# RWKV scan: the triangular inverse computed in 32x32 blocks instead of 64x64

## The reference, cut to what matters

```python
def rwkv7_scan(r, decay, k, v, kk, b, reverse):
    def step(S, inp):
        r_t, w_t, k_t, v_t, kk_t, b_t = inp
        sa = jnp.einsum('bhij,bhj->bhi', S, -kk_t)
        S = (S * w_t[:, :, None, :] + sa[..., None] * b_t[:, :, None, :]
             + v_t[..., None] * k_t[:, :, None, :])
        return S, jnp.einsum('bhij,bhj->bhi', S, r_t)
    S0 = jnp.zeros((B, H, N, N), r.dtype)
    _, y = lax.scan(step, S0, xs, reverse=reverse)
    return jnp.moveaxis(y, 0, 1)
```

## Time and profile before

| | us |
|---|---|
| median of 3 runs | 3494.51 (3489.61 to 3495.6) |
| the profiled execution | 3498.97 |
| its span, first to last instruction | 3497.2 |
| TensorE busy in the span | 3085.6 (88%) |
| the RWKV scan, 2467 to 2711 us | 244 |

### The profile page before, as it was taken

The page is one execution under the profiler, slowest core; times in us unless marked ns, Lnnn a source line. Parts: engine busy times, 40 slices in busy tenths (PEclk is TensorE's granted clock), DMA queues, the critical chain, the costliest instruction groups (busy, mean ns, idle before and its releaser), DMA issues. The chain is left out here.

```text
span 3497.2 us, 52679 instructions
## 1 busy us (share of the span) xinstructions
PE 3085.6 (88%) x19892; PEld 2517.5 (72%) x19892; DVE 1848.4 (53%) x2650; ACT 1038.8 (30%) x1592; POOL 1371.5 (39%) x701
## 2 busy tenths in 40 slices
PE   6976788999999999999999999792799766899977
PEld 4864565888888888878888888471799564588755
DVE  2025534986577777057777777546344832433023
ACT  2334312333333333221111111223222343333223
POOL 4440243345444444344444444340222333344433
PEclk8988888999999999999999999796899888899988
DMA  3320022244454554655555555123421101133321
GB/s 103 97 66 0 18 72 67 90 144 137 124 196 167 162 205 164 231 163 192 188 192 187 188 190 174 51 90 109 94 43 25 48 30 48 48 96 96 96 78 60
DMA packets 165895, 396.51 MB, mean 113 GB/s; under 512 B 53008, under 2 KB 53136, under 8 KB 164112
## 3 DMA queue, kind: packets, MB, share of 16 engines
q1 hardware_dynamic: 165776, 394.78, 35.1%
HBM read 314.77 MB, written 79.95 MB: 113 GB/s over the span
## 5 line engine op out<-in xcount | busy, mean ns | idle before, releaser
L158 POOL TENSOR_TENSOR weights_low<-weights_raw,weights_high 128x1024 fp32r<-128x1024 f32 x435 | 1133.7, 2606 | 1400.8 <-ACT weights_high L150 1400.8
L150 ACT ACTIVATE weights_high<-weights_raw 128x1024 fp32r<-128x1024 f32 x435 | 461.3, 1060 | 1944.0 <-PE psum L233 1867.9
L231 PE MATMUL psum<-expert_in_high,weights_high 128*128 128x512 f32 x1152 | 462.5, 401 | 21.0 <-POOL expert_in_low L327 10.5
L233 PE MATMUL psum<-expert_in_high,weights_low 128*128 128x512 f32 x1152 | 452.4, 393 | 0.0
L232 PE MATMUL psum<-expert_in_low,weights_high 128*128 128x512 f32 x1152 | 452.4, 393 | 0.0
L231 PE MATMUL psum<-coefficients_high,weights_high 128*128 128x512 f32 x1024 | 399.5, 390 | 7.3 <-DVE coefficients_low L1058 5.6
L233 PE MATMUL psum<-coefficients_high,weights_low 128*128 128x512 f32 x1024 | 398.5, 389 | 0.0
L232 PE MATMUL psum<-coefficients_low,weights_high 128*128 128x512 f32 x1024 | 398.4, 389 | 0.0
L1058 DVE TENSOR_TENSOR coefficients_low<-activation_in,coefficients_high 128x512 fp32r<-128x512 f32 x128 | 325.2, 2541 | 4.4
L231 PEld LDWEIGHTS psum<-expert_in_high,weights_high 128*128 128x128 f32 x1152 | 218.8, 190 | 71.7 <-issue 9.8
L233 PEld LDWEIGHTS psum<-expert_in_high,weights_low 128*128 128x128 f32 x1152 | 218.5, 190 | 46.4
(11 more groups left out here) (379 smaller groups left out, 5143.6 us busy)
## 6 DMA issues: line engine op xcount, KB each, us to landing
weights_raw<-in_weights SPq DMA_DIRECT2D x437, 512.0 KB, 3.6
expert_activations<-expert_activation SPq DMA_DIRECT2D x128, 256.0 KB, 4.2
coefficient_table<-table_stage SPq DMA_DIRECT2D x8, 4096.0 KB, 13.4
table_group<-coefficient_table SPq DMA_DIRECT2D x16, 2048.0 KB, 10.9
activation_in<-expert_activations SPq DMA_DIRECT2D x128, 256.0 KB, 3.7
chunk_vectors<-scan_vectors SPq DMA_DIRECT2D x8, 1280.0 KB, 8.5
scan_vectors<-scan_stage SPq DMA_DIRECT2D x8, 1024.0 KB, 4.1
residual_stream<-in_x SPq DMA_DIRECT2D x1, 2048.0 KB, 7.5
```

What stands on the lines that cost most here:

```text
L150: act.activation(d.hi[:, m % SPLIT, :], d.raw[:, m % RAW, :], ACT.Copy).then_inc(d.high, 1)
L158: pool.tensor_tensor(d.lo[:, m % SPLIT, :], d.raw[:, m % RAW, :], d.hi[:, m % SPLIT, :].bitcast(F32), ALU.subtract).then_inc(d.split, 1)
L231: pe.matmul(acc, w[0][:, cols], x[0], start=start, stop=False)
L233: return pe.matmul(acc, w[1][:, cols], x[0], start=False, stop=stop)
```

## The change

The inverse is computed to blocks of 32 tokens (`Q`), not 64. Levels 0 to 4 couple only tokens inside a 32-token block, so X is block-diagonal there, and only its two 32x32 blocks per problem are kept. With two problems per unit, four blocks lie on the four quarters of the partitions, and each product of a level is 4 units x 4 quarters of 32x32 matmuls (`blocks`), where quarter n uses rows and columns 32n to 32n + 31 of the array. X and X transposed lie in one tile `XX`; both increments are written next to each other into one bank, and VectorE adds both in one instruction. Level 0 makes both orientations by products with a 32x32 identity (`eye4`). The sixth level is replaced by two products for the one off-diagonal 32x32 block (`corner`): W_last = L's corner times the upper block of X, and dXT_last = W_last with the lower block. `XT`, 64 wide again, is made once by VectorE: the blocks multiplied by a 0/1 table (`place`), then the corner added by a multiply-add. GpSimd masks five levels instead of six and no longer waits for XT.

```diff
 C = 64
+Q = C // 2
...
-    while m < C:
+    while m < Q:
         levels.append(((s // (2 * m) == t // (2 * m)) & (s % (2 * m) < m) & (t % (2 * m) >= m)).astype(np.float32))
         m *= 2
     eye2 = (s == t).astype(np.float32)
+    eye4 = (np.arange(P)[:, None] % Q == np.arange(Q)[None, :]).astype(np.float32)
+    place = (np.arange(P)[:, None] // Q % 2 == np.arange(2)[None, :]).astype(np.float32)
...
-    LV = 6
+    LV = 5
     HALVES = (slice(0, C), slice(C, 2 * C))
+    BLOCKS = [(slice(n * Q, (n + 1) * Q), slice(n % 2 * Q, (n % 2 + 1) * Q)) for n in range(4)]
...
-        w = sb("L_level_times_X", [P, U, C])
-        X, XT = sb("X", [P, U, C]), sb("X_transposed", [P, U, C])
+        w = sb("L_level_times_X", [P, U, Q])
+        XX = sb("X_and_transposed_blocks", [P, 2, U, Q])
+        XT = sb("X_transposed", [P, U, C])
...
-                Bank(k, "rwkv", 4 * g, [("scores_b", 1)] + [(f"W{l}", 1) for l in lv] + [("sa", 1)]),
-                Bank(k, "rwkv", 4 * g + 1, [("scores_k", 1)] + [(f"dX{l}", 1) for l in lv[1:-1]] + [("y", 1)]),
-                Bank(k, "rwkv", 4 * g + 2, [("v_t", 1)] + [(f"dXT{l}", 1) for l in lv[1:]] + [("S", 1)]),
+                Bank(k, "rwkv", 4 * g, [("scores_b", 1)] + [(f"W{l}", 1) for l in lv] + [("W_last", 1), ("sa", 1)]),
+                Bank(k, "rwkv", 4 * g + 1, [("scores_k", 1)] + [(f"dX{l}", 1) for l in lv[1:]] + [("y", 1)]),
+                Bank(k, "rwkv", 4 * g + 2, [("v_t", 1), ("dXT_last", 1), ("S", 1)]),
...
                                 banks[g][0].full(pool, i, f"W{l - 2}")
-                            if l == 2:
-                                pool.wait_ge(ready[g], i + 1)
...
+
+                    def blocks(g, b, name, at, lhs, rhs, last=True):
+
+                        bank = banks[g][b]
+                        if at == 0:
+                            bank.free(pe, i, name)
+                        for u in range(H):
+                            for r, c in BLOCKS:
+                                mm = pe.matmul(bank.ps[r, at + u * Q:at + (u + 1) * Q], lhs(r, c, g * H + u),
+                                               rhs(r, c, g * H + u), start=True, stop=True)
+                        if last:
+                            mm.then_inc(bank.made, 1)
+
+                    def corner(g, b, name, lhs, rhs, up):
+
+                        bank = banks[g][b]
+                        bank.free(pe, i, name)
+                        for u in range(H):
+                            for first in (0, 2):
+                                src, dst = BLOCKS[first + up][0], BLOCKS[first + 1 - up][0]
+                                mm = pe.matmul(bank.ps[dst, u * Q:(u + 1) * Q], lhs(src, dst, g * H + u),
+                                               rhs(src, dst, g * H + u), start=True, stop=True)
+                        mm.then_inc(bank.made, 1)
+
+                    def X(r, c, u):
+                        return XX[r, 0, u, :]
+
+                    def X_turned(r, c, u):
+                        return XX[r, 1, u, :]
+
+                    def W(r, c, u):
+                        return w[r, u, :]
+
+                    def eye4(r, c, u):
+                        return consts("eye4")[r, :]
...
-                            product(g, 0, f"W{l}", C, [(lambda r, u: bl[r, l % 2, u, :], of(X) if l else eye)])
+                            blocks(g, 0, f"W{l}", 0, lambda r, c, u: bl[r, l % 2, u, c], X if l else eye4, last=l > 0)
+                            if l == 0:
+                                blocks(g, 0, "W0", H * Q, eye4, lambda r, c, u: bl[r, 0, u, c])
                         for g in range(2):
                             if l == 0:
                                 continue
                             banks[g][0].taken(pe, i, f"W{l}")
-                            if l == 1:
-                                pe.wait_ge(ready[g], i + 1)
-                            else:
-                                banks[g][2].taken(pe, i, f"dXT{l - 1}")
-                            if l < LV - 1:
-                                product(g, 1, f"dX{l}", C, [(of(XT), of(w))])
-                            product(g, 2, f"dXT{l}", C, [(of(w), of(XT))])
+                            blocks(g, 1, f"dX{l}", 0, X_turned, W, last=False)
+                            blocks(g, 1, f"dX{l}", H * Q, W, X_turned)
+                    for g in range(2):
+                        banks[g][1].taken(pe, i, f"dX{LV - 1}")
+                        corner(g, 0, "W_last", lambda src, dst, u: L[src, u, Q:C], lambda src, dst, u: XX[src, 0, u, :], False)
+                    for g in range(2):
+                        banks[g][0].taken(pe, i, "W_last")
+                        corner(g, 2, "dXT_last", lambda src, dst, u: w[src, u, :], lambda src, dst, u: XX[src, 1, u, :], True)
...
-                        banks[g][2].taken(pe, i, f"dXT{LV - 1}")
+                        banks[g][2].taken(pe, i, "dXT_last")
...
-                                take(g, 0, f"W{l}", w[:, half(g), :], view(g, 0, C))
+                                take(g, 0, f"W{l}", w[:, half(g), :], view(g, 0, Q))
+                        for g in range(2):
+                            take(g, 0, "W_last", w[:, half(g), :], view(g, 0, Q))
...
                     for g in range(2):
-                        dve.wait_ge(lev[g], i * LV + 1)
-                        dve.tensor_tensor(XT[:, half(g), :], bl[:, 0, half(g), :], mask("eye2"), ALU.add).then_inc(ready[g], 1)
                         banks[g][0].full(dve, i, "W0")
-                        dve.tensor_tensor(X[:, half(g), :], view(g, 0, C), mask("eye2"), ALU.add).then_inc(banks[g][0].read, 1)
+                        src = banks[g][0].ps[:, 0:2 * H * Q].rearrange("p (a u t) -> p a u t", a=2, u=H)
+                        dve.tensor_tensor(XX[:, :, half(g), :], src,
+                                          consts("eye4")[:, None, None, :].to_broadcast([P, 2, H, Q]),
+                                          ALU.add).then_inc(banks[g][0].read, 1)
...
                         for g in range(2):
-                            if l < LV - 1:
-                                banks[g][1].full(dve, i, f"dX{l}")
-                                if l == 1:
-                                    banks[g][0].taken(dve, i, "W0")
-                                else:
-                                    banks[g][1].taken(dve, i, f"dX{l - 1}")
-                                dve.tensor_tensor(X[:, half(g), :], view(g, 1, C), X[:, half(g), :],
-                                                  ALU.add).then_inc(banks[g][1].read, 1)
-                            banks[g][2].full(dve, i, f"dXT{l}")
+                            bank = banks[g][1]
+                            bank.full(dve, i, f"dX{l}")
                             if l == 1:
-                                dve.wait_ge(ready[g], i + 1)
+                                banks[g][0].taken(dve, i, "W0")
                             else:
-                                banks[g][2].taken(dve, i, f"dXT{l - 1}")
-                            dve.tensor_tensor(XT[:, half(g), :], view(g, 2, C), XT[:, half(g), :],
-                                              ALU.add).then_inc(banks[g][2].read, 1)
+                                bank.taken(dve, i, f"dX{l - 1}")
+                            src = bank.ps[:, 0:2 * H * Q].rearrange("p (a u t) -> p a u t", a=2, u=H)
+                            dve.tensor_tensor(XX[:, :, half(g), :], src, XX[:, :, half(g), :], ALU.add).then_inc(bank.read, 1)
+                    for g in range(2):
+                        banks[g][1].taken(dve, i, f"dX{LV - 1}")
+                        dve.tensor_tensor(XT[:, half(g), :].rearrange("p u (b t) -> p u b t", b=2),
+                                          XX[:, 1, half(g), None, :].to_broadcast([P, H, 2, Q]),
+                                          consts("place")[:, None, :, None].to_broadcast([P, H, 2, Q]),
+                                          ALU.mult).then_inc(ready[g], 1)
+                    for g in range(2):
+                        bank = banks[g][2]
+                        bank.full(dve, i, "dXT_last")
+                        dve.wait_ge(ready[g], i + 1)
+                        dve.scalar_tensor_tensor(out=XT[:, half(g), Q:C], in0=view(g, 2, Q), scalar=consts("place")[:, 0:1],
+                                                 in1=XT[:, half(g), Q:C], op0=ALU.mult, op1=ALU.add).then_inc(bank.read, 1)
```

More of the change, by code:

```diff
@@ L420, in layout_constants @@
              ("iota", iota), ("ones", ones), ("half", half), ("upper", upper), ("upper_eq", upper_eq),
-             ("eye2", eye2), ("levels", np.concatenate(levels, 1)), ("chunk_start", start)]
+             ("eye2", eye2), ("eye4", eye4), ("place", place), ("levels", np.concatenate(levels, 1)), ("chunk_start", start)]
     where, at = {}, 0
@@ L1703, in rwkv_scan @@
         lev = [sem(f"L_levels_masked{g}") for g in range(2)]
-        ready = [sem(f"X_transposed_started{g}") for g in range(2)]
```

(1 more changed line is left out.)

## The result

The kernel after takes 3629.22 us (median of 4 runs, 3622.9 to 3633.92), the kernel before 3495.06 on the same chip: ratio 1.0385, 95% interval 1.0365 to 1.0405. Forecast was 3463. The kernel got slower by 134 us, and the range of 3450 to 3500 was missed by 129.

The account below looks back on a forecast made before the run. TensorE was taken to bound the scan. Saving 4.1 us a chunk, 33 in eight, less 2 for tile size, gives 31: 3498.97 profiled becomes 3468, less 4.5 for the median, 3463 us; own range 3455 to 3474, within 3450 to 3500.

Parts of the forecast that it names:

- Spacing of 16.4 ns a matmul with four quarters at once: Inverse's 32x32 products: four tiles run at once, 8.2 ns a record, 16.4 ns a matmul against 58.3 now.
- Rival 1: Inverse's products: a 32-column record costs what one of 64 does, 29.1 ns a matmul; kernel 3497 us; chance 0.09.
- rival 2: Inverse's products: only two tiles ever run at once, 32.8 ns a matmul; kernel 3506 us; chance 0.09.
- The level as a sum of eight terms, 2.19 us: Inverse's levels: W, copy, dX products, add and the waits between them sum to 2.19 us a level against 3.03.
- the 31 us: Whole scan: 33 us saved over eight chunks, less 2 us for the change of tile size.
- Change of tile size, 0.27 us a chunk: TensorE switching 64x64 to 32x32 and back, twice a chunk: 0.27 us a chunk, 2 us in all.
- Rival 3, the clock falls in the gaps: TensorE in the scan, some 73% busy in the levels: 1.2 GHz there gives about 3506 us, over all up to 3600; chance 0.05.
- Rival 4, instructions arrive too slowly: Scan's instruction packets: if one took 2 us, the levels would last 15 us; kernel 3490 us; chance 0.07.
- 1.1 us each ... and 1.1 is below 1.6: Scan's instruction packets: each takes 1.1 us, while the new levels need one per 1.6 us.
- my 2 us: Assumed time of one instruction packet in the scan, with which the levels would last 15 us.
- Nothing stops TensorE for it now: Scan of the kernel before: TensorE has no stops for instructions, held against slow arrival of instructions.
- All other stages the same: Sign in the profile after: outside the scan, some 31 us shorter, every stage stays the same.

Follow-up runs that it names:

- four_units_a_matmul: Kernel after, with one matmul of 128 moving columns for four units, all using the first unit's weights: 3475.78 us, ratio 0.9943.
- before_vector_transposes: Kernel before, with X transposed by VectorE in 32x32 blocks instead of a third product in levels 1 to 4, and no level 0 product: 3484.8 us, ratio 0.9981.
- two_units_a_matmul: Kernel after, with one matmul of 64 moving columns for two units, both using the first unit's weights: 3514.38 us, ratio 1.0048.
- after_vector_transposes: Kernel after, with the transposed blocks of levels 1 to 4 made by VectorE instead of the second half of the dX products: 3575.0 us, ratio 1.0245.
- the probe: Kernel before, with constant-table matmuls added behind the scan: 32x32 in straight line and in loops, then 64x64: 3633.51 us, one run.
- split_columns: Kernel before, with each 64x64 matmul of the inverse's W, dX and dXT written as two of 32 moving columns: 3695.76 us, ratio 1.0565.

## Why the prediction was wrong

The mean chunk of the seven whole ones, against the sum 3.73 x blocks + 3.6 (no loops in these):
```
kernel                    records  blocks  sum    measured
four_units_a_matmul        1392     5.44   23.9   26.6
before_vector_transposes   1472     5.75   25.0   27.2
before                     1792     7      29.7   30.4
two_units_a_matmul         1856     7.25   30.6   32.2
after_vector_transposes    2240     8.75   36.2   38.9
after                      2752    10.75   43.7   45.2
```
Work that differs in tiles, columns and engines lies near one line from 7 blocks up; in the top two rows the chain of the levels (24.6 to 26.5 us by its parts) is about as long or longer. The sum is 0.7 to 2.7 us low throughout. Some blocks take 3.9 to 4.1 us, and the clock has a part in it; the two weren't told apart.

By the prediction's own steps:
- *Spacing of 16.4 ns a matmul with four quarters at once*: right. 8.7 ns a record, 17.4 a matmul, in the kernel after and in the probe's loop at full clock. Rival 1 (14.6 ns a record) and rival 2 are out. The rule of the Trainium skill that stood with rival 1 (TensorEngine Tiling (Array Packing), section Performance Considerations) is not what the 32x32 tiles show; on 64x64 tiles split_columns agrees with it, since there a record of 32 columns cost what one of 64 does.
- *The level as a sum of eight terms, 2.19 us*: right where the code arrives in time (2.04 with four units, with the same copies and adds), and with it the 31 us. The copy took 278 ns against 0.28 us, the add 425. The chunk was 26.6 us with four units, against 26.5 forecast.
- *Change of tile size, 0.27 us a chunk*: at most that. In the kernel after W0's first record starts 0.15 us behind the last transpose's, before it was 0.05.
- *Rival 3, the clock falls in the gaps*: it fell, to 0.50 for 27 to 31 of some 45 us of each chunk, each time with the first long stop of the levels or behind it. With four units, where only three gaps in the scan are over 1 us, it was 0.98. Its own share in the levels is small: at half clock the 128 records of a block are done in some 2 us of the 3.7. But the 64x64 products right behind the levels ran at half clock too, 507 matmul records in the scan at some 53 ns where 29 is usual. That is an estimate of at most 12 us of the 118, and less where the code would have come late anyway.
- *Rival 4, instructions arrive too slowly*, chance 0.07 and 3490 us: this is what happened, with the sign that the prediction gave for it ("issue" inside the products), and the step that failed is its price, "1.1 us each ... and 1.1 is below 1.6". The 1.1 us are how long a packet's transfer takes by the profile. What sets the supply is the time from one block to the next, some 3.73 us, and no row gives it, because packets that come as they are used up say nothing of how fast they could come. With 3.73 for my 2 us the same sum would have said it: 1920 records are 7.5 blocks, 28 us where the inverse took 15.9, so +12 us a chunk and +97 in all (measured +118 in the scan).
- "Nothing stops TensorE for it now" was read rightly and proved nothing: a block's work lasted 3.73 us as well (64 matmuls x 58.3 ns). The earlier trace rows has 57 packets in 244 us; that is one every 4.3 us, and the change asks for one per 1.6.
- *"All other stages the same"*: this failed too, by the 15 us of the coefficient stage. With four units the scan was as forecast and the kernel still took 3476 us, not 3463.

## What to carry to other kernels

Before splitting products into more and smaller ones, count TensorE's records and divide by 256: if a block's work gets below some 3.7 us (29 ns a matmul record), the supply of code sets the time in runs like these, whatever the tiles do. A profile that is bound by TensorE at just that rate has no room left that way. What helps is fewer instructions: more columns for each, work given to VectorE, or a loop of up to 1400 records that turns many times; one that turns only four times pays its first turn in full and lets no code arrive meanwhile.

## What the hardware showed that was not expected

- A block of 256 TensorE instructions comes every 3.5 to 4.1 us, also with nothing else on the DMA queues (3.70 us on average in the probe).
- On 64x64 tiles a record with 32 moving columns and 64 weight columns is spaced as one with 64 moving columns (28.8 to 29.1 ns); on 32x32 tiles, with 32 weight columns, it is 8.7. Four tiles are at work there and not two, which gives a factor of 2 of the 3.3; the rest goes with the size of the tile, and whether its rows or its weight columns do it wasn't separated.
- The clock was halved for 48 to 51 us at a time while TensorE was busy 57.9 of 60 us. Each fall came just behind a stop of 0.7 to 2.1 us. Why it stayed low so long isn't shown.
- VectorE's transpose of 128x256 in 32x32 blocks takes 418 ns, as an add of that size.
